# Moving the context key and value products of the joint attention behind the latent feed-forward

## The chip, the cores and the metric

One Trainium2 chip, one NeuronCore of it. A core has TensorE (PE: matrix products from SBUF into PSUM), VectorE (DVE), ScalarE (ACT) and GpSimd (POOL), each with its own in-order instruction queue, and SyncE (SP), whose queue issues most of the DMAs. SBUF is the working memory; PSUM has eight banks of 128 partitions by 2 KB. Engines wait for each other through semaphores only. The metric is the device time of one execution in microseconds (us), the median of three runs.

## The reference

Two networks in a row on 512 tokens of width 1024, everything in float32. The first block runs two layers, each with a mixer (latent attention, pooling, spatial gating) and a feed-forward. In a layer's mixer, keys and values of the attention come from a normed vector of 256, and `sg_mixer` takes another projection `v` of the same rows:

```python
p = jnp.einsum('bsd,dn->bsn', rmsnorm(x, mix_norm[l]), w_in[l])
ckv = rmsnorm(h_kv, kv_norm_g)            # keys and values, a part of p
z = jax.nn.gelu(h_uv)                     # u and v of the gating, another part of p
```

The second block works on the 512 latent tokens and 256 context tokens. Its layer 0 has a recurrent mixer and a feed-forward for both; its layer 1 has a joint attention for the latents, in which the context gives keys and values only:

```python
h_lat = modulate(x, norm_g[l, 0], sh1, sc1)       # rmsnorm times gain, plus shift
h_ctx = modulate(ctx, norm_g[l, 0], csh1, csc1)
q_c, k_c, v_c = prep(h_ctx, False)                # products with w_qkv; q and k rmsnormed per head
q_l, k_l, v_l = prep(h_lat, True)                 # the same with rotary angles
k_all = jnp.concatenate([k_c, k_l], axis=1)
y_lat = blocked_attention(q_l, k_all, v_all) @ w_out
x = x + g1 * rmsnorm_2(y_lat, norm_g[l, 1])
x = x + g2 * rmsnorm_2(swiglu(modulate(x, ...), ffn_w_in[l], ffn_w_out[l]), norm_g[l, 3])
```

## The kernel before

Activations lie transposed in SBUF: a tensor is eight tiles (k = 0 to 7) of 128 features by 512 tokens (256 for the context). Each float32 operand of a product is held as two factors, a rounded one (`H`) and the rest (`L`), and each product is three matrix products: high by high, high by low, low by high.

Weights come in chunks, of 1 MB mostly. SP loads a chunk into `raw` (two buffers, by the parity of the chunk's number), ACT rounds it into `WH` (function `hi(c)`, line 844), POOL makes `WL = raw - WH` (line 773). All three have two buffers; `hi(c)` waits until PE has used chunk c-2, and SP loads chunk c when the low part of c-2 is made. The order of the chunks is one list (`names`, lines 473 to 482), which all engines follow. `rounded` (line 902) makes the high factors of a normed tensor, and its argument `late` places one `hi` among them.

The program is written out by hand per engine; there is no scheduler. A prefix names the stage: `b0`, `b1` the layers of the first block, `c` and `t` the context's and the latents' part of the recurrent layer, `k` the context's keys and values of the joint attention, `m` the joint attention and its feed-forward. Names of steps: `n1` and `n2` the norms ahead of a mixer and a feed-forward, `y1` and `y2` those behind them, `sq` squares, `sum`, `root`, `rec` and `bc` the sum over features, its root, reciprocal and spread to all partitions. The statistics of a norm go ACT (square), PE (sum by a product with ones), ACT (root), DVE (reciprocal), PE (spread, lines 3070 and 3147), DVE (the normed tensor).

Around the change:

- The latent feed-forward `t` has 22 tiles of gate and up products in four quarters (6, 6, 6, 4), and behind each quarter the down products. `key_values` exists as a generator on PE, ACT and DVE, and one step of it is taken after each tile of the last quarters. On PE it has the 96 products of the context's keys (48, into bank `S[0]`) and values (48, into `S[1]`), each 128 by 256, ahead of the last quarter's down products, and then the sums and the spread of the keys' norm between these. Its two weight chunks `k.kv` come ahead of the last down chunks `t.dn3`.
- Behind the feed-forward PE takes the statistics of `t.y2`; DVE adds the normed result to `xT` in 8 pairs of instructions (`add_to`, line 2418: a product into `ht`, a sum into `xT`); ACT squares each new tile, PE sums the squares (`row_sums`, line 3100), and the norm `m.n1` follows. Its opening (line 3014) takes products tile by tile as the factors `hH` and `hL` come. Where PE would wait it multiplies identity matrices (`keep_busy`, line 3053, the rows with `SS<-ident`).
- In `first_mixing` of the layers `b0` and `b1` PE projects the gating's `v` in four parts (24 products each, 128 by 256, into `G[0]` to `G[3]`), with `spread_roots("nkv")` between the second and third.
- At the norm `t.n1` of the latents in the recurrent layer, ACT makes `hi` of the second column chunk ahead of the first high factor.

## Time and profile before

| what | value |
|---|---|
| median of three runs | 3058.39 us (3052.99 to 3061.25) |
| the profiled execution | 3058.06 us, of which its span 3056.3 us |
| mean granted TensorE clock | 0.989 of full |
| PE, busy | 2979.7 us, 97% |
| PE, weight loads | 2479.6 us, 81% |
| DVE, ACT, POOL busy | 56%, 39%, 40% |
| DMA | 323.81 MB, mean 106 GB/s |

The share of PE in the chain that ended last is 89%, that of DVE 7%. Times in the trace are counted from the start of the span; 1.8 us of the execution lie outside it. A row that begins with a start, a length and PE stands for one instruction or for several merged ones (`x16`, weight loads counted beside products). A matmul's length holds the way through the array, so the time that one takes of the engine is the distance to the next start. In brackets is the idle time of the engine ahead of the row, and what ended it. The granted clock has two levels here, 2.4 and 1.2 GHz.

### The profile page before, as it was taken

To read this page: it belongs to the slowest core of one execution; us is meant where nothing else is said; L and a number is where in the kernel's file an instruction comes from. 1 tells how busy PE (TensorE), PEld (TensorE's weight loads), DVE (VectorE), ACT (ScalarE), POOL (GpSimd) and SP (SyncE) were. 2 spreads that over 40 slices of the span, in tenths; PEclk is the share of its full clock that TensorE was granted. 3 is DMA by queue.
4 is the path that set the end of the run, shared out by engine and by line. 5 is a ranking of instruction groups with operands and counts; after the bars stand their busy time and mean duration, and the time that the engine had idled before them with its cause. 6 is when DMAs were issued, how large, how long until landed. Compare 5 with 4: busy or idle time off the path is not lost.

```text
span 3056.3 us, 41128 instructions
## 1 busy us (share of the span) xinstructions
PE 2979.7 (97%) x16292; PEld 2479.6 (81%) x16292; DVE 1718.6 (56%) x2812; ACT 1180.8 (39%) x1826; POOL 1237.1 (40%) x584
## 2 busy tenths in 40 slices
PE   8999999999999999999999999999999999999999
PEld 7668888776688888888888998878878779888887
DVE  4656677846563553654428866676684478431113
ACT  4553222246445333234436655531223445332222
POOL 4223444532276333324444554444444320244442
PEclk9999999999999999999999999999999999999999
DMA  7214554522245223223333343355653220123331
GB/s 133 66 56 128 167 174 149 174 63 68 75 132 148 87 70 93 74 68 132 106 90 99 115 124 105 124 153 170 199 161 110 70 69 1 42 76 102 100 98 67
DMA packets 468112, 323.81 MB, mean 106 GB/s; under 512 B 90200, under 2 KB 435424, under 8 KB 467408
## 3 DMA queue, kind: packets, MB, share of 16 engines
q1 hardware_dynamic: 463152, 309.55, 34.4%
q10 hardware_dynamic: 2656, 6.30, 0.6%
q0 software_dynamic: 2112, 5.32, 0.5%
q8 instruction: 130, 2.13, 0.3%
q14 instruction: 62, 0.51, 0.1%
HBM read 315.85 MB, written 5.24 MB: 105 GB/s over the span
## 4 chain that ended last, share of the span: by engine, by line
PE 89%; DVE 7%; ACT 2%; issue 1%; POOL 1%; DMA 0%; DVEq 0%; ACTq 0%; POOLq 0%
PE G L2997 13%; PE G L3006 13%; PE G L3007 12%; PE G L3011 12%; PE G L3252 6%; PE G L3253 5%; PE G L3257 5%; PE G L3024 3%; PE G L4173 1%; PE SS L3381 1%; PE G L3487 1%; PE MM L3381 1%; PE G L3473 1%; DVE acc L1783 1%; PE G L3418 1%
## 5 line engine op out<-in xcount | busy, mean ns | idle before, releaser
L773 POOL TENSOR_TENSOR WL<-raw,WH 128x1024 fp32r<-128x1024 f32 (+1 forms) x520 | 1194.1, 2318 | 1709.0 <-ACT WH L844 1709.0
L844 ACT ACTIVATE WH<-raw 128x1024 fp32r<-128x1024 f32 (+1 forms) x520 | 493.2, 996 | 582.4 <-PE G L3257 374.4
L3006 PE MATMUL G<-hH,WH 128*128 128x512 f32 x1520 | 595.2, 392 | 0.7 <-ACT xtok L1583 0.7
L3007 PE MATMUL G<-hL,WH 128*128 128x512 f32 x1520 | 591.9, 389 | 0.0
L3011 PE MATMUL G<-hH,WL 128*128 128x512 f32 x1520 | 359.9, 389 | 0.0
L3006 PEld LDWEIGHTS G<-hH,WH 128*128 128x128 f32 x1520 | 285.4, 188 | 64.6 <-issue 3.3
L3011 PEld LDWEIGHTS G<-hH,WL 128*128 128x128 f32 x1520 | 285.3, 188 | 59.2
L3007 PEld LDWEIGHTS G<-hL,WH 128*128 128x128 f32 x1520 | 285.4, 188 | 58.4
L1783 DVE SCALAR_TENSOR_TENSOR acc<-adaw,cvec,acc 128x512 f32<-128x512 f32 x280 | 286.4, 1075 | 4.2
L1812 DVE TENSOR_TENSOR FH<-silu,G 128x512 fp32r<-128x512 f32 x44 | 30.2, 687 | 234.2 <-PE G L3011 178.6
L2997 PE MATMUL G<-hH,WH 128*128 128x512 f32 (+1 forms) x416 | 160.0, 385 | 0.0
L2997 PE MATMUL G<-hL,WH 128*128 128x512 f32 (+1 forms) x416 | 157.4, 378 | 0.0
L2997 PE MATMUL G<-hH,WL 128*128 128x512 f32 (+1 forms) x416 | 157.3, 378 | 0.0
L3252 PE MATMUL G<-FH,WH 128*128 128x512 f32 x352 | 140.6, 399 | 0.3 <-DVE xT L1828 0.3
L3253 PE MATMUL G<-FL,WH 128*128 128x512 f32 x352 | 138.2, 392 | 0.0
L928 ACT ACTIVATE silu<-G 128x512 f32<-128x512 f32 x44 | 26.3, 598 | 274.0 <-PE G L3011 265.0
L1812 DVE TENSOR_TENSOR m_FH<-m_silu,G 128x512 fp32r<-128x512 f32 x22 | 15.1, 687 | 188.9 <-PE G L3011 183.3
L2997 PEld LDWEIGHTS G<-hH,WH 128*128 128x128 f32 x416 | 79.0, 190 | 15.2 <-issue 1.1
L2997 PEld LDWEIGHTS G<-hL,WH 128*128 128x128 f32 x416 | 79.0, 190 | 14.6 <-issue 0.7
L2997 PEld LDWEIGHTS G<-hH,WL 128*128 128x128 f32 x416 | 78.8, 189 | 14.5
L3257 PE MATMUL G<-FH,WL 128*128 128x512 f32 x352 | 85.0, 389 | 0.0
L3024 PE MATMUL G<-hH,WH 128*128 128x512 f32 (+1 forms) x160 | 65.3, 408 | 17.7 <-DVE hL L2464 7.6
(832 smaller groups left out, 5973.6 us busy)
## 6 DMA issues: line engine op xcount, KB each, us to landing
raw<-ffn_w_in_in SPq DMA_DIRECT2D x264, 256.0 KB, 3.4
adaw<-ada_w_in SPq DMA_DIRECT2D x48, 1024.0 KB, 5.2
raw<-ab_w_in_in SPq DMA_DIRECT2D x128, 256.0 KB, 3.0
raw<-ffn_w_out_in SPq DMA_DIRECT2D x96, 256.0 KB, 2.9
raw<-w_gate_in SPq DMA_DIRECT2D x88, 256.0 KB, 3.3
raw<-w_up_in SPq DMA_DIRECT2D x88, 256.0 KB, 3.4
raw<-w_down_in SPq DMA_DIRECT2D x64, 256.0 KB, 3.0
raw<-w_in_in SPq DMA_DIRECT2D x40, 256.0 KB, 3.7
```

Source lines behind the costliest of these rows:

```text
L773: nc.gpsimd.tensor_tensor(low(c)[:, cut], raw[c % 2][:, cut], high(c)[:, cut].bitcast(F32), ALU.subtract)\
L844: nc.scalar.activation(high(c)[:, cut], raw[c % 2][:, cut], ACT.Copy).then_inc(weights_hi, 1)
L1783: V.scalar_tensor_tensor(sums[:, b, i, :], weights[h % 2][:, k, :], col, sums[:, b, i, :], ALU.mult, ALU.add)\
L2997: last = mm(dst, x, y, start=(k == 0 and j == 0), stop=(k == K - 1 and j == 2))
L3006: mm(dst, view(high(c), k), xh, start=(k == 0 and not (joint and i)), stop=False)
L3007: mm(dst, view(high(c), k), xl, start=False, stop=False)
L3011: last = mm(dst, view(low(c), k), X(k)[0], start=False, stop=(k == K - 1 and not (joint and i == 0)))
L3024: last = mm(dst, x, y, start=(k == order[0] and j == 0 and not (joint and i)), stop=(k == K - 1 and j == 2 and not (joint and i == 0)))
L3252: mm(dst, part(high(c), k, cols, o), xh, start=(k == 0 and not (joint and i)), stop=False)
L3253: mm(dst, part(high(c), k, cols, o), xl, start=False, stop=False)
L3257: last = mm(dst, part(low(c), k, cols, o), X(k)[0], start=False, stop=(k == count - 1 and not (joint and i == 0)))
L3381: mm(SCORES[i][:, :], qT[:, h, i * P:i * P + P], kT[:, h, :], start=True, stop=True).then_inc(pe_done, did("pe", f"{n}.sc{4 * h + i}"))
```

## The change

- Order of chunks: `k.kv` comes behind `t.dn3`, and ahead of `m.qkv`.
- PE: the 96 products leave the generator. `sums_with_keys` issues them one by one (`fill`) behind the feed-forward: 24 ahead of the sums of `t.y2`, 6 ahead of its spread, 18 behind it, then 4 behind each of the eight row sums of `m.n1`, 6 ahead of its column sums, 6 behind them and 4 behind its spread. The keys go to `S[1]`, the values to `G[2]`. The identity products of these places go; the eight ahead of the opening stay.
- The keys' norm: its sums follow the opening of `m.qkv` on PE, its spread and DVE's products lie in the second head pair; the factors `c_kH` and `c_kL` are made one pair later.
- ACT: `hi(k.kv + 1)` comes behind the last square of `t.y2`, `hi(m.qkv)` behind the second square of `m.n1`, `hi(m.qkv + 1)` ahead of the fourth high factor (before: ahead of the first). The copies of the keys out of PSUM come behind the fifth square, those of the values behind the sixth high factor.
- DVE: the product of each pair in `add_to("t", 2)` goes to PSUM (`G[0]`, `G[3]`) in place of `ht`.
- `first_mixing`: `spread_roots("nkv")` is moved from the third `v` part to the fourth.
- `t.n1`: `hi` of the second column chunk is moved from the first high factor to the third.

In three places the order of the instructions is shown, as a listing of the two programs has it (engine's order, line, operation, output and inputs, shape). On PE, from the end of the latent feed-forward to the second row sum of `m.n1`, before:

```order
L3257 MATMUL G<-t_FH,WL_68 128x512 x8
L3059 MATMUL SS<-ident 128x128 x8
L3092 MATMUL MM<-ones,rstd 128x1 x4
L3095 MATMUL MM<-ones,sq 128x1 x4
L3059 MATMUL SS<-ident 128x128 x2
L3147 MATMUL MM<-ident,ncol 128x128 x4
L3059 MATMUL SS<-ident 128x128 x8
L3103 MATMUL MM<-sq,ones 1x512
L3059 MATMUL SS<-ident 128x128
```

And in the changed kernel (`c_kH`, `c_kL` are the factors of the normed context, `WH_54` and `WH_57` the two weight buffers):

```order
L3263 MATMUL G<-t_FH,WL_68 128x512 x8
L3980 MATMUL SS<-c_kH,WH_54 128x256
...
L3098 MATMUL MM<-ones,rstd 128x1 x4
L3101 MATMUL MM<-ones,sq 128x1 x4
L3980 MATMUL SS<-c_kH,WH_54 128x256
...
L3153 MATMUL MM<-ident,ncol 128x128 x4
L3980 MATMUL SS<-c_kH,WH_54 128x256
...
L3109 MATMUL MM<-sq,ones 1x512
L3994 MATMUL G<-WH_57,c_kH 128x256
L3994 MATMUL G<-WL_68,c_kH 128x256
L3994 MATMUL G<-WH_57,c_kL 128x256
L3994 MATMUL G<-WH_57,c_kH 128x256
```

The identity products are gone, context products stand in their places, and four of the values' products follow the first row sum. On ACT, from the end of the feed-forward to the high factors of `m.n1`, before:

```order
L844 ACTIVATE WH_54<-raw_52 128x1024 x2
L870 ACT_TABLE_LOAD
L870 ACTIVATE MM<-MM,eps 128x4
L894 ACTIVATE rstd<-t_y_181 128x512
L894 ACTIVATE sq<-t_y_181 128x512 x7
L870 ACTIVATE MM<-MM,eps 128x4
L853 ACTIVATE sq<-xT 128x512 x8
L861 ACTIVATE rstd<-MM 1x512
L870 ACTIVATE ncol<-MM,eps 128x4
L844 ACTIVATE WH_57<-raw_53 128x1024 x2
L911 ACTIVATE hH<-SS,mod 128x512
L911 ACTIVATE hH<-MM,mod 128x512
```

And in the changed kernel:

```order
L890 ACTIVATE sq<-t_y_181 128x512 x7
L840 ACTIVATE WH_57<-raw_53 128x1024 x2
L866 ACT_TABLE_LOAD
L866 ACTIVATE MM<-MM,eps 128x4
L849 ACTIVATE sq<-xT 128x512 x2
L840 ACTIVATE WH_54<-raw_52 128x1024 x2
L849 ACTIVATE sq<-xT 128x512 x3
L1542 ACTIVATE kc<-SS 128x256 x2
L849 ACTIVATE sq<-xT 128x512 x3
...
L866 ACTIVATE ncol<-MM,eps 128x4
...
L913 ACTIVATE hH<-SS,mod 128x512
L840 ACTIVATE WH_57<-raw_53 128x1024 x2
```

The table load and a pair of weight halves now stand behind the last square of `t.y2`, another pair behind the second square of `m.n1`, and the third pair, which stood ahead of the first high factor, behind the third. On PE in layer `b0` (and alike in `b1`), around the spread of `nkv`, with the banks' numbers, before:

```order
L2997 MATMUL G1<-WL0_62,hH_50 128x256
L2997 MATMUL G1<-WH0_54,hL_51 128x256
L3070 MATMUL MM<-nrow_89,ident_77 128x128 x4
L2997 MATMUL G2<-WH0_54,hH_50 128x256
L2997 MATMUL G2<-WL0_62,hH_50 128x256
```

And in the changed kernel:

```order
L3003 MATMUL G2<-WL0_62,hH_50 128x256
L3003 MATMUL G2<-WH0_54,hL_51 128x256
L3076 MATMUL MM<-nrow_89,ident_77 128x128 x4
L3003 MATMUL G3<-WH0_54,hH_50 128x256
L3003 MATMUL G3<-WL0_62,hH_50 128x256
```

The spread now stands ahead of the part that goes to `G3`, 24 products later than before.

The diff, cut to its core and without its repeated parts:

```diff
@@ -476,8 +476,7 @@
         names += [("c.o", 4, SLOT), *columns_of("t"), *halves("c"), ("t.o", 4, SLOT)]
-        latent = halves("t")
-        names += [*latent[:-1], ("k.kv", 2, SLOT), latent[-1]]
+        names += [*halves("t"), ("k.kv", 2, SLOT)]
         names += [("m.qkv", 6, SLOT), ("m.o", 4, SLOT)]
@@ -896,6 +892,12 @@
                     (added_square if n in ADDED else square)(n, k, src(k), fresh)
+                    if n == "t.y2" and k == K - 1:
+                        hi(first["k.kv"] + 1)
+                    if n == "m.n1" and k == 1:
+                        hi(first["m.qkv"])
+                    if n == "m.n1" and k == 4:
+                        keys_out()
                 stats_before[0] = f"{n}.sum"
@@ -1532,23 +1534,18 @@
                 rounded("k.n1", KD, PC.kH, None, TC, shift("k", 0), temp=sq)
-                yield
-                c = first["k.kv"]
-                hi(c + 2)
+            def keys_out():
                 for g in range(2):
                     act.wait_ge(pe_done, at("pe", "k.k1"))
-                    nc.scalar.activation(kc[:, g, :], S[0][:, g * TC:g * TC + TC], ACT.Copy).then_inc(act_done, did("act", f"k.k{g}"))
-                hi(c + 3)
+                    nc.scalar.activation(kc[:, g, :], S[1][:, g * TC:g * TC + TC], ACT.Copy).then_inc(act_done, did("act", f"k.k{g}"))
+            def values_out():
                 for k in range(TC // P):
                     act.wait_ge(pe_done, at("pe", "k.v1"))
-                    nc.scalar.activation(vc[:, k, :], S[1][:, k * 2 * P:k * 2 * P + 2 * P], ACT.Copy).then_inc(act_done, did("act", f"k.v{k}"))
-                yield
-                act.wait_ge(act_done, at("act", "k.k1"))
-                act.wait_ge(dve_done, at("dve", f"k.n1.L{KD - 1}"))
-                nc.scalar.activation(sq[:, 0, :], kc[:, :, :].rearrange("p g t -> p (g t)"), ACT.Square).then_inc(act_done, did("act", "k.nk.sq"))
-                yield
-                root("k.nk", 2 * (TC // P), P)
-                stats_before[0] = "k.nk.sum"
+                    nc.scalar.activation(vc[:, k, :], G[2][:, k * 2 * P:k * 2 * P + 2 * P], ACT.Copy).then_inc(act_done, did("act", f"k.v{k}"))
 
@@ -1593,7 +1590,7 @@
             projected("c", PC.y, TC, KD, ((3, final_roots), (5, lambda: turned_context(2))))
-            rounded("t.n1", KD, hH, f"c.o{KD - 1}", T, shift("t", 0), late=first["t.ab"] + 1)
+            rounded("t.n1", KD, hH, f"c.o{KD - 1}", T, shift("t", 0), late=first["t.ab"] + 1, late_at=2)
             turned_context(3)
@@ -1607,7 +1604,10 @@
             stats("m.n1", KD, lambda k: xT[:, k, :], lambda k: act.wait_ge(dve_done, at("dve", f"t.x2.{k}")))
-            rounded("m.n1", KD, hH, f"t.up{FT - 1}", T, shift("m", 0), late=first["m.qkv"] + 1)
+            rounded("m.n1", KD, hH, f"t.up{FT - 1}", T, shift("m", 0), late=first["m.qkv"] + 1, late_at=3, then=lambda k: values_out() if k == 3 else None)
+            act.wait_ge(act_done, at("act", "k.k1"))
+            nc.scalar.activation(sq[:, 0, :], kc[:, :, :].rearrange("p g t -> p (g t)"), ACT.Square).then_inc(act_done, did("act", "k.nk.sq"))
+            stats_before[0] = "k.nk.sum"
             c = first["m.qkv"]
@@ -1634,14 +1634,17 @@
 
-            for g in range(2):
-                act.wait_ge(dve_done, at("dve", f"k.kn{g}"))
-                nc.scalar.activation(c_kH[:, g, :], kc[:, g, :], ACT.Copy).then_inc(act_done, did("act", f"m.cH{g}"))
             for i in range(NH // 2):
...
                     root(f"m.p{i - 1}", 2 * P, P)
+                else:
+                    root("k.nk", 2 * (TC // P), P)
                 head(2 * i + 1)
+                if i == 1:
+                    for g in range(2):
+                        act.wait_ge(dve_done, at("dve", f"k.kn{g}"))
+                        nc.scalar.activation(c_kH[:, g, :], kc[:, g, :], ACT.Copy).then_inc(act_done, did("act", f"m.cH{g}"))
                 hi(c + 2 + i)
@@ -2419,14 +2422,15 @@
                     dve.wait_ge(dve_done, here())
-                    V.scalar_tensor_tensor(temp[:, k % 2, 0:N], y[:, k, :], g(k), bank[:, 0:N], ALU.mult, ALU.mult)\
+                    step = (G[0], G[3])[k % 2][:, 0:N] if (n, which) == ("t", 2) else temp[:, k % 2, 0:N]
+                    V.scalar_tensor_tensor(step, y[:, k, :], g(k), bank[:, 0:N], ALU.mult, ALU.mult)\
                         .then_inc(dve_done, did("dve", f"{n}.d{which}.{k}"))
...
                     dve.wait_ge(dve_done, here())
-                    V.tensor_tensor(x[:, k, :], x[:, k, :], temp[:, k % 2, 0:N], ALU.add).then_inc(dve_done, did("dve", f"{n}.x{which}.{k}"))
+                    V.tensor_tensor(x[:, k, :], x[:, k, :], step, ALU.add).then_inc(dve_done, did("dve", f"{n}.x{which}.{k}"))
 
@@ -3308,8 +3314,9 @@
                     if k == 2:
+                        pe.wait_ge(act_done, at("act", f"{n}.prow1"))
+                    if k == 3:
                         spread_roots(f"{n}.nkv")
-                        pe.wait_ge(act_done, at("act", f"{n}.prow1"))
                     cut = bass.ds(k * P, P)
@@ -3959,28 +3966,74 @@
                 yield
+            def key_products():
                 c = first["k.kv"]
-                X = features(PC.kH, PC.kL, TC)
                 ready("k.n1", KD)
...
                 for g in range(2):
-                    three(S[0][:, g * TC:g * TC + TC], KD, weights_of(c, blocks(2 * P)(g)), X).then_inc(pe_done, did("pe", f"k.k{g}"))
-                tally.also("pe", f"used.{c}")
+                    weights = weights_of(c, blocks(2 * P)(g))
+                    for q in range(KD):
+                        (wh, wl), (xh, xl) = weights(q), (PC.kH[:, q, :], PC.kL[:, q, :])
+                        for j, (x, y) in enumerate(((wh, xh), (wh, xl), (wl, xh))):
+                            last = mm(S[1][:, g * TC:g * TC + TC], x, y, start=(q == 0 and j == 0), stop=(q == KD - 1 and j == 2))
+                            if q == KD - 1 and j == 2:
+                                last.then_inc(pe_done, did("pe", f"k.k{g}"))
+                            if g == 1 and q == KD - 1 and j == 2:
+                                tally.also("pe", f"used.{c}")
+                            yield
                 chunk(c + 1)
+                pe.wait_ge(dve_done, at("dve", "t.down3.6"))
+                weights = weights_of(c + 1, lambda w, q: w[:, q * 2 * P:(q + 1) * 2 * P])
                 for k in range(TC // P):
                     cut = bass.ds(k * P, P)
-                    three(S[1][:, k * 2 * P:k * 2 * P + 2 * P], KD, lambda q: (PC.kH[:, q, cut], PC.kL[:, q, cut]),
-                          weights_of(c + 1, lambda w, q: w[:, q * 2 * P:(q + 1) * 2 * P])).then_inc(pe_done, did("pe", f"k.v{k}"))
-                tally.also("pe", f"used.{c + 1}")
-                yield
-                yield
+                    for q in range(KD):
+                        (wh, wl), (xh, xl) = weights(q), (PC.kH[:, q, cut], PC.kL[:, q, cut])
+                        for j, (x, y) in enumerate(((xh, wh), (xh, wl), (xl, wh))):
+                            last = mm(G[2][:, k * 2 * P:k * 2 * P + 2 * P], x, y, start=(q == 0 and j == 0), stop=(q == KD - 1 and j == 2))
+                            if q == KD - 1 and j == 2:
+                                last.then_inc(pe_done, did("pe", f"k.v{k}"))
+                            if k == 1 and q == KD - 1 and j == 2:
+                                tally.also("pe", f"used.{c + 1}")
+                            yield
+            def fill(products, count):
+                for _ in range(count):
+                    next(products, None)
+            def sums_with_keys():
+                products = key_products()
+                fill(products, 24)
+                pe.wait_ge(dve_done, at("dve", stats_before[0]))
+                added_columns("t.y2", KD)
+                fill(products, 6)
+                pe.wait_ge(dve_done, at("dve", "t.y2.rec"))
+                to_all(M[1][:, :], 0).then_inc(pe_done, did("pe", "t.y2.bc"))
+                fill(products, 18)
+                for k in range(KD):
+                    row_sums("m.n1", k)
+                    fill(products, 4)
+                fill(products, 6)
+                row_columns("m.n1")
+                fill(products, 6)
+                pe.wait_ge(dve_done, at("dve", "m.n1.rec"))
+                to_all(M[1][:, :], 0).then_inc(pe_done, did("pe", "m.n1.bc"))
+                fill(products, 4)
+                stats_before[0] = "m.n1.rec"
+            def keys_sum():
                 pe.wait_ge(act_done, at("act", "k.nk.sq"))
-                pe.wait_ge(dve_done, at("dve", stats_before[0]))
                 for t in range(4):
...
                 stats_before[0] = "k.nk.rec"
-                yield
+            def keys_root():
                 pe.wait_ge(dve_done, at("dve", "k.nk.rec"))
@@ -4130,6 +4183,8 @@
                     if b == 0:
+                        if i == 1:
+                            keys_root()
                         head_sums(i - 1)
...
                             swap(i - 2)

```

## Rows read from the trace of the kernel before

**Rows 1.** The page's first part: engine, busy us (share), instructions.
```profile
PE 2979.7 (97%) x16292; PEld 2479.6 (81%) x16292; DVE 1718.6 (56%) x2812; ACT 1180.8 (39%) x1826; POOL 1237.1 (40%) x584
```

**Rows 2.** Instructions in time order (start us, length us, engine, idle before), PE, key products.
```profile
2351.26 3.79 PE L3011 MATMUL G<-hH,WL 128*128 128x512 f32 x16
2355.43 0.35 PE L2997 MATMUL SS<-c_kH,WH 128*128 128x256 f32 x1 [0.38 <-ACT ht L928]
...
2366.88 0.39 PE L3252 MATMUL G<-t_FH,WH 128*128 128x512 f32 x1
```

**Rows 3.** Instructions in time order, VectorE, beside those products.
```profile
2356.78 0.69 DVE L1815 TENSOR_TENSOR t_FL<-G,t_FH 128x512 fp32r<-128x512 f32 x1
```

**Rows 4.** Instructions in time order, PE, from the latent feed-forward's end to the opening.
```profile
2391.58 2.02 PE L3059 MATMUL SS<-ident 128*128 128x128 f32 x16 [0.87 <-DVE t_y L1828]
...
2395.83 1.16 PE L3147 MATMUL MM<-ident,ncol 128*128 128x128 f32 x8
...
2409.77 1.02 PE L3103 MATMUL MM<-sq,ones 128*1 128x512 f32 x2
2410.72 0.49 PE L3059 MATMUL SS<-ident 128*128 128x128 f32 x2
2411.47 1.05 PE L3109 MATMUL MM<-ones,rstd 1*128 1x1 f32 x8 [0.26 <-ACT rstd L861]
...
2416.68 0.47 PE L3024 MATMUL G<-hH,WH 128*128 128x512 f32 x1 [0.66 <-ACT hH L911]
```

**Rows 5.** Instructions in time order, ScalarE, same stretch.
```profile
2391.47 0.63 ACT L894 ACTIVATE sq<-t_y 128x512 f32<-128x512 f32 x1 [0.28 <-DVE t_y L1828]
...
2401.55 0.63 ACT L853 ACTIVATE sq<-xT 128x512 f32<-128x512 f32 x1 [0.88 <-DVE xT L2429]
...
2417.36 0.69 ACT L911 ACTIVATE hH<-SS,mod 128x512 fp32r<-128x512 f32 x1 [0.82 <-DVE SS L1750]
```

**Rows 6.** Instructions in time order, PE, value products of layers 0 and 1.
```profile
79.51 1.16 PE L3070 MATMUL MM<-nrow,ident 128*128 128x128 f32 x8 [3.40 <-DVE nrow L1723]
...
677.66 1.17 PE L3070 MATMUL MM<-nrow,ident 128*128 128x128 f32 x8 [3.39 <-DVE nrow L1723]
```

**Rows 7.** Instructions in time order, ScalarE and PE, opening of the latent columns.
```profile
1425.21 1.99 ACT L844 ACTIVATE WH<-raw 128x1024 fp32r<-128x1024 f32 x2
...
1428.71 0.47 PE L3024 MATMUL G<-hH,WH 128*128 128x512 f32 x1 [3.82 <-POOL WL L773]
```

**Rows 8.** The chain of waits (start us, length us, what).
```profile
80.67 5.76 PE G L2997 x48
...
678.83 7.23 PE G L2997 x48
...
1428.71 12.78 PE G L3024 x48
```

**Rows 9.** Instructions in time order, ScalarE: a table load ahead of a root.
```profile
1373.71 1.28 ACT L870 ACT_TABLE_LOAD   x1
1375.16 0.25 ACT L870 ACTIVATE SS<-SS,eps 128x16 f32<-128x16 f32 x1 [0.16 <-PE SS L3701]
```

**Rows 10.** Instructions in time order, VectorE, same stretch.
```profile
2420.13 0.74 DVE L1739 SCALAR_TENSOR_TENSOR hL<-MM,mod,hH 128x512 fp32r<-128x512 f32 x1
```

**Rows 11.** Instructions in time order, GpSimd, around the opening.
```profile
2413.84 4.71 POOL L773 TENSOR_TENSOR WL<-raw,WH 128x1024 fp32r<-128x1024 f32 x2 [29.93 <-ACT WH L844]
```

**Rows 12.** Instructions on one tile, the rotary table swap: its load.
```profile
DMA to landing us min/median/max: 4.5/4.5/4.5
```

**Rows 13.** Instructions of one line: ns min/median/max, first and last start, shape.
```profile
L1828 DVE TENSOR_TENSOR xT<-xT,G x64: 686/687/691, 315.4 to 1389.3; 128x512 f32<-128x512 f32 x64
...
L2429 DVE TENSOR_TENSOR ctxT<-ctxT,ht x8: 424/425/1932, 1478.3 to 1488.7; 128x256 f32<-128x256 f32 x8
```
**Rows 14.** Gating of `b0` in time order: DVE's last product on v, PE's first use.
```profile
93.43 1.23 DVE L1926 TENSOR_TENSOR vg<-vg,sgrow 128x1024 f32<-128x1024 f32 x1
...
109.29 1.12 PE L3355 MATMUL MM<-b_s,bsel 33*128 33x512 f32 x2
```

24 lines of the change are left out of this document (11 added, 13 removed).

## The prediction

> **What bounds the kernel now.** I read the page first: PE is busy for 97% of the span [rows 1], while its weight loads fill 81%. So nothing is gained beside PE; time can only come from work that PE no longer does on its own account, from waits of PE, and from stretches in which it runs at the lower clock. Then I read the time-ordered views of the four places that the change touches, and looked there for idle time in brackets. Three things are to be seen.
>
> (a) The 96 context products stand alone on PE between the last up product and the first down product: from the idle 0.38 us ahead of 2355.43 to 2366.88 [rows 2], 11.83 us, or 0.119 us a product. Nothing but DVE's last low factor (from 2356.78, 0.69 us long [rows 3]) is under way beside them.
>
> (b) Behind the feed-forward, from 2391.58 to 2416.68 [rows 4], PE waits for a chain through DVE and ACT: sums, root, eight tiles at 1.51 us each (ACT's square 0.63 us and its idle 0.88 us [rows 5]), sums, root, first factors. Of this PE's share is small, and identity products fill the rest. That stretch is 25.1 us long, the products need 11.4.
>
> (c) In `b0` and `b1` PE idles 3.40 and 3.39 us ahead of the spread of `nkv` [rows 6], and at `t.n1` 3.82 us ahead of the opening [rows 7]. The stretches behind two of these are slow: 48 products of 256 columns take 5.76 us in `b0` and 7.23 us in `b1` [rows 8].
>
> **Part 1, the products leave the feed-forward's end.** The down products then start 11.83 us earlier. What is late next: they need the latest low factor of the feed-forward only at their 13th product. A product of 512 columns takes 0.23 us (16 in 3.79 [rows 2]), so that is 2.7 us after their start at about 2355.0, at 2357.7; DVE has it at 2356.78 + 0.69 = 2357.47 [rows 3]. The cover is 0.2 us; I count no wait. The sums and the spread of the keys' norm also leave the down products and come back one for one among the latents' heads: 0. Removed: **11.8 us**.
>
> **Part 2, the products go between the statistics.** They cost only where they or their companions are longer than what they stand beside. All that follows is serial, so lateness adds up.
> - First fill: 24 products, 24 x 0.119 = 2.9 us, for eight identity products of 1.9 us (2.02 with the way through the array [rows 4]). The sum of `t.y2` comes 1.0 later. Six products (0.8) stand for two identities (0.6) ahead of the spread, whose reciprocal comes late by the same 1.0: +0.1.
> - ACT's table load moves to just ahead of this root. At 1373.71 such a load ran before the wait of its root ended: it took 1.28 us, and the root still waited 0.16 us for PE [rows 9]. Here ACT ends its last square at 2392.1 (2391.47 + 0.63 [rows 5]); with 2.0 for the weight halves and 1.3 for the load it is ready at 2395.4. The root is wanted 0.5 ahead of the old spread (2395.83 [rows 4]) plus 1.0, at 2396.3. Hidden.
> - `hi(m.qkv)` behind the second square is 2.0 us long (1.99 [rows 7]) in a queue that has 0.88 us free in a step [rows 5]. The third square comes 2.0 - 0.9 = 1.1 to 1.2 late. ACT then catches up, PE doesn't: a row sum takes 0.95 of PE (2409.77 to 2410.72 [rows 4]), four products 0.48 and the change back to them some 0.08, together 1.51 us, just the pace of DVE's step. So the last row sum is **1.2** late.
> - Behind the last row sum PE issues ten products before the column sums: 0.95 + 1.28 = 2.23, where before 1.70 went by (2409.77 to 2411.47): +0.5. Six instead of two identities ahead of the second spread: +0.2. Four more ahead of the opening: 0.5 of the 0.66 us for which PE idled [rows 4]: 0.
> - `hi(m.qkv + 1)` now delays the fourth high factor. The third is written 2417.36 to 2418.05 [rows 5], then 2.0 us of weights and 0.7 of the factor, to 2420.8; DVE took that factor at 2420.13 [rows 10], and PE follows DVE tile by tile: +0.7.
> - The loads of the rotary tables stand on POOL behind the low part of that chunk. It ran from 2413.84 for 4.71 us [rows 11]; it would now start at 2419.2, the last load be issued at 2424.9 and land 4.5 later [rows 12], at 2429.4. PE waits for it behind the opening and the keys' sums, at about 2429.6. Hidden with 0.2 to spare; I count 0 and keep up to 2 for the range.
>
> Sum of this part: 1.0 + 0.1 + 1.2 + 0.5 + 0.2 + 0.7 = **3.7 us back**.
>
> **Part 3, the product of each pair in PSUM.** DVE's instruction lengths for one operand in PSUM: 0.686 to 0.691 over 64 instructions, also while POOL makes low parts; a sum of two SBUF tiles beside POOL (`ctxT`, 256 columns) takes 0.42 but once 1.93 [rows 13]. Before, POOL was quiet for 29.9 us ahead of 2413.84 [rows 11]; now two low parts, four instructions, lie beside DVE's pairs. With the product in PSUM I count 0; bounds: -0.5 if the pair gets shorter, and 4 x 1.5 = 6.0 if each of POOL's four instructions stops DVE once. Zero is next to the row with PSUM.
> The Trainium skill (SBUF — State Buffer, section "Who interferes with whom") has this as a rule: a VectorE instruction with two SBUF inputs contends with a GpSimd instruction that reads SBUF, and one with at most one does not. By that rule the sum has 0 here, and would have up to 6.0 more with `ht` kept; the rows agree with it.
>
> **Part 4, the spread of `nkv`.** The 24 products (2.9 us at 0.120) now run where PE idled 3.40 and 3.39 us; 0.5 us of the wait is left, the spread comes when it came, and PE is 2.9 earlier behind it: 2 x 2.85 = **5.7 us**. What is next late: DVE's work on `v` ended at 93.43 + 1.23 = 94.7 and PE wanted it at 109.29 [rows 14], 14.6 us later; it has slack for all of it. Behind the wait in `b1` the same 48 products took longer than in `b0`, at the lower clock for a part; with 0.5 us of idleness I expect it not to fall: 7.23 - 5.76 = **1.5 us**. In `b0` a wait as long left the clock up, so this is likely and not sure.
>
> **Part 5, `t.n1`.** The first high factor waited behind `hi` (1425.21, 1.99 us [rows 7]). Now it starts at 1425.3, and PE's opening at 1426.8 in place of 1428.71: 1.9. The `hi` comes before the third factor, which costs 0.4. The opening itself took 12.78 us [rows 8], against 48 x 0.23 = 11.0: 1.7 at the lower clock behind an idle time of 3.82. With 2.0 us of it left I count 1.0 of that: 1.9 - 0.4 + 1.0 = **2.5 us** (bounds 1.0 and 3.2).
>
> **The sum.** Against the profiled execution: 3058.06 - 11.8 + 3.7 - 5.7 - 1.5 - 2.5 = 3058.06 - 17.8 = 3040.3 us. The median of the runs is 0.33 above that execution, so 3040.6; I say **3040.5 us**, 0.59% below.
>
> **Rivals.**
> - *The chain in the seam is longer than counted.* For: PE's and DVE's pace in the row sums are equal to 0.01 us, the cover of the tables' load is 0.2 us, and each late item adds up. If the row-sum step takes 1.8 us, 8 x 0.3 = 2.4 more; with 2 us of waiting for the tables, 1 for a POOL stop, and 1.5 for the clock kept low in `b1`: 3040.5 + 6.9 = about 3047.5. Against: each step has a row of its own length.
> - *The waits in `b0`, `b1` and `t.n1` come back later.* For: PE at 97% [rows 1] leaves hardly any waits to see, so the slack of the others isn't visible either. Then only parts 1 and 2 count: 3058.4 - 8.1 = 3050.3, no measurable change. Against: everything behind these places is released relative to PE, DVE and ACT start as much earlier, and no load or clock of its own holds them.
> - *DVE's pairs in PSUM are stopped, slower in the end.* Place: the 16 instructions of `add_to` between the spread and the last row sum. Price 1.5 us for each one stopped [rows 13]. All 16 would be 24 us: 3040.5 + 24 = 3064.5. It decides from 12 stopped on (18 us). For: `G[0]` and `G[3]` are PSUM banks beside the one that PE now fills, and POOL works beside it. Against: 64 instructions of that kind never went over 0.691, and POOL has only four instructions there.
> - *The change does not do what it says:* PE might still wait for the products' weights. The tightest are those of the values: `hi(k.kv + 1)` runs behind the square that ends at 2392.1, the first low half starts at 2393.2 and POOL takes 4.7 us [rows 11], to 2397.9; the 49th product follows the first row sum at about 2401. If they came 4 us late, 1 us; I leave it inside the range.
>
> **How the numbers follow.** My forecast 73%, the longer seam 14%, the waits that come back 10%, PSUM 3%. What this kernel's measurement can tell from no change is 0.3%, 9.2 us, that is 3049.2. The forecast's own range is 3035 to 3046: from all of part 2 hidden (3036.8) and the clock's gifts larger by 2, to the clock gains of 2.5 absent and 3 of spread between runs. Towards the rivals I take 3034 to 3050. Faster by over 0.3%: 0.73 + 0.12 + 0.01 = 0.86; same: 0.02 + 0.09 = 0.11; slower 0.03.
>
> **What would show it.** In the profile of the changed kernel: the down products of the last quarter directly behind the last up product, with no idle time (part 1); from the end of the last down product to the opening some 29 us in place of 25 to 26, with the third square of `xT` late by 1.2 and the last row sum still so (part 2); DVE's pairs at 0.75 and 0.69 us beside POOL (part 3); waits of 0.5 us ahead of the spreads of `nkv`, and 48 products behind none of them slow (part 4); the opening of `t.n1` 2 us after the last product before it (part 5). I am wrong if PE's idle time grows elsewhere by more than 3 us, if the seam takes over 33 us, or if the low clock shows in new places.

## The result and the profile after

| | before | after |
|---|---|---|
| median, first comparison | 3059.19 us (4 runs, 3052.99 to 3061.25) | 3034.45 us (4 runs, 3031.76 to 3036.84) |
| ratio, 95% interval | | 0.9922 [0.9904, 0.9940] |
| repeated later, median | 3057.45 us (9 runs) | 3037.80 us (5 runs) |
| ratio, 95% interval | | 0.9938 [0.9924, 0.9951] |
| profiled execution; its span | 3058.06; 3056.3 us | 3032.47; 3030.7 us |
| mean granted clock in it | 0.989 | 0.992 |

The change makes the kernel 0.6 to 0.8% faster. The forecast was 3040.5 us (0.59% less), with a range of 3034 to 3050: the sign and the mechanism are right, and the measured gain is larger. All 9 runs of the changed kernel together have a mean of 3035.9 us, the 46 runs of the kernel before 3058.4: 22.5 us less, good to about 2 us by the spread of the runs, where the sum said 17.8.

The page after [rows 1]: PE is busy for 2961.0 us in place of 2979.7.

```profile
PE 2961.0 (98%) x16236; PEld 2462.2 (81%) x16236; DVE 1721.3 (57%) x2812; ACT 1179.5 (39%) x1826; POOL 1237.6 (41%) x584
```

PE in time order, from the last up products to the products behind the opening (start, length, engine, line, ...; in brackets the idle time before it). It answers to [rows 2, 4]:

```profile
2335.73 3.79 PE L3017 MATMUL G<-hH,WL 128*128 128x512 f32 x16
2339.35 0.39 PE L3258 MATMUL G<-t_FH,WH 128*128 128x512 f32 x1
...
2362.25 0.36 PE L3980 MATMUL SS<-c_kH,WH 128*128 128x256 f32 x1 [0.90 <-DVE t_y L1831]
...
2365.16 0.95 PE L3098 MATMUL MM<-ones,rstd 128*128 128x1 f32 x8
...
2367.66 1.05 PE L3153 MATMUL MM<-ident,ncol 128*128 128x128 f32 x8
...
2370.94 1.02 PE L3109 MATMUL MM<-sq,ones 128*1 128x512 f32 x2 [0.18 <-ACT sq L849]
...
2372.56 1.02 PE L3109 MATMUL MM<-sq,ones 128*1 128x512 f32 x2
...
2374.87 1.02 PE L3109 MATMUL MM<-sq,ones 128*1 128x512 f32 x2 [0.64 <-ACT sq L849]
...
2382.97 1.02 PE L3109 MATMUL MM<-sq,ones 128*1 128x512 f32 x2
...
2385.29 1.05 PE L3115 MATMUL MM<-ones,rstd 1*128 1x1 f32 x8
...
2387.09 1.05 PE L3153 MATMUL MM<-ident,ncol 128*128 128x128 f32 x8
...
2390.59 0.47 PE L3030 MATMUL G<-hH,WH 128*128 128x512 f32 x1 [0.19 <-ACT hH L913]
...
2402.52 0.95 PE L4031 MATMUL MM<-ones,sq 128*128 128x1 f32 x8
```

The down products follow the last up product (2335.73 + 16 x 0.227 = 2339.35) with no idle time. From the first fill (2362.25) to the opening (2390.59) are 28.34 us; before it was 25.10 [rows 4]. The third row sum waited 0.64 us for its square (2374.87), and from then on the row sums are 1.62 us apart, where before they were 1.51 apart. Four more rows of the kernel before are needed for the terms below: its sum of `t.y2`, its first row sum, its second spread, and the first product behind its opening.

```profile
2393.44 0.95 PE L3092 MATMUL MM<-ones,rstd 128*128 128x1 f32 x8
...
2399.31 1.02 PE L3103 MATMUL MM<-sq,ones 128*1 128x512 f32 x2 [0.53 <-DVE ht L2422]
...
2413.08 1.16 PE L3147 MATMUL MM<-ident,ncol 128*128 128x128 f32 x8
...
2428.16 0.39 PE L2997 MATMUL G<-hH,WH 128*128 128x512 f32 x1
```

The eighth row sum came 10.46 us after the first (2399.31 to 2409.77) and comes 12.03 after it now (2370.94 to 2382.97). The opening took 11.48 us (2416.68 to 2428.16) and takes 11.93 (2390.59 to 2402.52). ScalarE and GpSimd beside it; the two long ACT rows are the chunks that were moved there [rows 5, 7, 11]:

```profile
2372.31 1.99 ACT L840 ACTIVATE WH<-raw 128x1024 fp32r<-128x1024 f32 x2
2374.20 1.22 ACT L849 ACTIVATE sq<-xT 128x512 f32<-128x512 f32 x2
...
2391.85 2.00 ACT L840 ACTIVATE WH<-raw 128x1024 fp32r<-128x1024 f32 x2
...
2373.43 4.71 POOL L769 TENSOR_TENSOR WL<-raw,WH 128x1024 fp32r<-128x1024 f32 x2 [4.89 <-ACT WH L840]
```

The two spreads of `nkv` and the opening of `t.n1` [rows 6 to 8]. The idle time ahead of them is 0.52, 0.52 and 1.93 us; before it was 3.40, 3.39 and 3.82:

```profile
76.92 1.16 PE L3076 MATMUL MM<-nrow,ident 128*128 128x128 f32 x8 [0.52 <-DVE nrow L1726]
...
672.22 1.16 PE L3076 MATMUL MM<-nrow,ident 128*128 128x128 f32 x8 [0.52 <-DVE nrow L1726]
...
1416.45 0.47 PE L3030 MATMUL G<-hH,WH 128*128 128x512 f32 x1 [1.93 <-DVE hL L1742]
```

### The profile page after: what moved, and what is told of

The parts are those of the page before. It is cut to its first block, busy times and chain, and to the rows that moved or that the text cites. A ratio compares the mean times of both kernels' runs of the same rounds, so it can differ in the third digit from the quotient of the medians.

```text
span 3030.7 us, 41013 instructions
## 1 busy us (share of the span) xinstructions
PE 2961.0 (98%) x16236; PEld 2462.2 (81%) x16236; DVE 1721.3 (57%) x2812; ACT 1179.5 (39%) x1826; POOL 1237.6 (41%) x584
## 4 chain that ended last, share of the span: by engine, by line
PE 89%; DVE 7%; ACT 2%; issue 1%; POOL 1%; DMA 0%; DVEq 0%; ACTq 0%; POOLq 0%
PE G L3003 13%; PE G L3012 13%; PE G L3013 13%; PE G L3017 13%; PE G L3258 5%; PE G L3259 5%; PE G L3263 5%; PE G L3030 3%; PE G L4228 1%; PE SS L3388 1%; PE G L3494 1%; PE MM L3388 1%; PE G L3480 1%; DVE acc L1786 1%; PE G L3832 1%
## 5 line engine op out<-in xcount | busy, mean ns | idle before, releaser
L3003 PE MATMUL G<-hH,WH 128*128 128x512 f32 (+1 forms) x416 | 160.1, 385 | 0.0
L3258 PEld LDWEIGHTS G<-FH,WH 128*128 128x128 f32 x352 | 66.6, 189 | 18.2 <-issue 1.8
```

Source lines behind the costliest of these rows:

```text
L3003: last = mm(dst, x, y, start=(k == 0 and j == 0), stop=(k == K - 1 and j == 2))
L3258: mm(dst, part(high(c), k, cols, o), xh, start=(k == 0 and not (joint and i)), stop=False)
```

## Where the time went

I laid the two traces over each other: the same instruction is looked up in both, and the difference of its start is followed through the program. Each step in it is a place where time went.

| place | step after minus before, us | forecast |
|---|---|---|
| the start, ahead of any edit | -2.5 | 0 |
| spread of `nkv`, `b0` | -3.0 | -2.85 |
| spread of `nkv`, `b1`, clock included | -4.3 | -4.35 |
| opening of `t.n1` | -1.9 | -1.5 |
| its length (12.78 both times) | 0.0 | -1.0 |
| behind 1920 and behind 2000 (before's times) | -2.4, -0.9 | 0 |
| last up product to first down product | -12.0 | -11.8 |
| keys' norm out of the down products | -1.8 | among the heads one for one |
| first fill to the opening | +3.2 | +3.0 |
| the opening itself | +0.45 | +0.7 |
| keys' norm among the heads | +1.8 | |
| behind 2655 | -2.2 | 0 |
| all others, single steps of up to 1.5 of both signs | 0.0 | 0 |

The rows with a forecast sum to -17.6; the parts that were counted came out within 0.5 us each, except the clock of `t.n1`. The other -8 us stand at places that no edit touches. There the same instructions are under way, at another clock. The largest of the steps that cancel is such a place too: 3.4 us at the low clock at 888 us of the changed kernel cost 1.5, where the kernel before has none, and the slow stretch at 853 us of the kernel before is shorter in the changed one, for about as much. Two places of the -8 us by windows (window, length, PE busy (instructions), granted clock, DMA share, GB/s); first before, then after:

```profile
5.00:30.00 25.00, 20.37 (x107) 0.93 1.01 213
1980.00:2010.00 30.00, 25.99 (x133) 0.77 0.00 1
```

```profile
5.00:30.00 25.00, 20.04 (x118) 1.00 1.00 214
1965.00:1995.00 30.00, 24.88 (x137) 0.89 0.00 1
```

## The experiments

**1. Parts 4 and 5 alone.** To the kernel before:

```diff
@@ first_mixing, PE @@
                     if k == 2:
-                        spread_roots(f"{n}.nkv")
                         pe.wait_ge(act_done, at("act", f"{n}.prow1"))
+                    if k == 3:
+                        spread_roots(f"{n}.nkv")
@@ t.n1, ACT @@
-            rounded("t.n1", ..., late=first["t.ab"] + 1)
+            rounded("t.n1", ..., late=first["t.ab"] + 1, late_at=2)
```

> The kernel before with parts 4 and 5 alone (the spread of nkv one value product group later in b0 and b1, the second weight chunk of t.n1 ahead of the third high factor). Theory (waits given back for good, each -2.88 in b0 and -2.88 in b1, and -1.9 at t.n1): the program behind t.n1 runs 7.7 us earlier than before, -9.2 with the slow stretch behind the wait of b1 gone; time about 3059.2 - 9 = 3050. Rival (the waits come back later as other waits): shift of the last third back near 0, time 3059. Rival (the clock, not the waits, is what differed between the two executions): the shifts at places that no edit touches (start of the program, 1850 to 1942 us, 2660 us) differ again, by other amounts and signs than in the changed kernel, 1 to 3 us at a place.

Measured: 3044.51 us (5 runs) against 3057.07 (9), ratio 0.9955 [0.9942, 0.9967]. The steps are -2.95, -4.3 and -1.9, as the theory has them, and nothing comes back: "the waits come back" falls. But 3057.07 - 3044.51 = 12.6 us, 3.4 more than the 9.2 counted. In the trace this excess is once more at untouched places: -2.2 at 1942 us and -0.9 at 2009. The second rival, that the clock at untouched places would differ by other amounts and signs than in the changed kernel, is borne out in half: these two steps are the same in both, but the start (0 here, -2.5 there) and the place behind 2655 us (+0.4 here, -2.2 there) differ.

**2. Parts 1 to 3 alone**: the changed kernel with the two edits of experiment 1 taken back.

> The changed kernel with parts 4 and 5 undone, so parts 1 to 3 alone. Theory (12.0 us of products taken out of the feed-forward's end, 3.7 given back between the statistics): the opening of m.n1 stands 8.3 us earlier than before relative to the last up product, PE idles 3.4 us ahead of both spreads of nkv and 3.8 ahead of the opening of t.n1; time about 3059.2 - 8.3 = 3051. Rival (the two halves help each other, by the clock or by earlier loads): less than 8 from the seam, time 3053 or more, and the two halves together less than the changed kernel's 24.7. By the theory the halves sum to 17.4 and the remaining 7 are the granted clock of the executions.

Measured: 3046.79 us (5 runs), ratio 0.9965 [0.9952, 0.9977], 10.3 us by medians. The step from the last up product to behind the heads' first products is -8.4 us in the trace. The halves add up within their spread: 12.6 + 10.3 = 22.9 by medians and 24.3 by means, the whole change has 22.5 by its mean. In this kernel the waits of `b0` and `b1` are there again (3.4 us); the spreads behind them took 2.08 and 1.52 us, against 1.16 at the high clock, and the 48 products 6.17 and 6.92.

**3. The kernel before, a second time.**

> The kernel before, unchanged, profiled a second time. Theory (the 8 us beyond the counted parts are the granted clock, whose slow stretches fall in other places from one execution to the next): the program is the same, yet stretches of PE at the lower clock stand in other places than in the first profile, with shifts of 1 to 3 us at single places and the mean clock between 0.989 and 0.992. Rival (the slow stretches belong to the program): the same places as in the first profile, shifts under 0.5 us everywhere.

The chain of waits (start, length, what), two rows of the first execution, to which the 5.76 us at 80.67 of [rows 8] belong, and four of the second:

```profile
90.30 19.07 PE G L2997 x84
...
1942.34 4.97 DVE hL L2819 x2
```

```profile
80.03 2.07 PE MM L3070 x8
82.10 6.19 PE G L2997 x48
92.16 19.07 PE G L2997 x84
...
1941.85 4.98 DVE hL L2819 x2
```

One program, and yet it is 1.9 us behind itself at 92 us and 0.5 ahead at 1942. Behind the wait of `b0` the spread and the products together took 1.16 + 5.76 = 6.92 us in one [rows 6, 8] and 2.07 + 6.19 = 8.26 in the other: 1.3 us for the low clock. So the prediction's "in `b0` a wait as long left the clock up" held for the one execution that it was read from. The theory stands in part: of the slow stretches most have the same place in both executions, and some come, go or change their length, a microsecond or two at a place.

**4. The changed kernel, a second time**, five runs.

> The changed kernel, unchanged, timed and profiled again beside the version with halves. Theory (between executions of one program the low clock falls in other places): stretches at the start, behind 1400 us, at 1930 us and behind 2640 us differ from the first profile by 0.5 to 2.5 us each, while the seam from the last down product to the end of the opening is the same to 0.2 us; median 3034 to 3037. Rival (the first profile's places are fixed by the program): all shifts under 0.5 us.

Measured: 3037.80 us, 3033.65 to 3039.16, 0.8 above the range expected. In the traces it is 3.4 us later than the first from 35 us on, 1.2 later from 1437 us on, and has no lasting step over 0.15 us from there to the end; the seam is the same to 0.1 us. The theory's places were too many: differences at the start and at 840 to 1440 us, none at 1930 and 2640. That the mean clock is 0.992 in both profiles of the changed kernel, and 0.989 and 0.988 in both of the kernel before, says that a part of the 8 us is the change's after all. The sums of (1 - granted clock) x length over the profiles say the same: 35.1 and 35.5 us before, 25.3 and 25.3 after. Four profiles are few, and both of the changed kernel are of executions faster than its mean. But every run has its granted clock listed: (1 - clock) x span has a mean of 35.8 us over 42 runs of the kernel before (those of the first comparison have none) and of 28.7 over the 9 of the changed one. That is 7.1 us less at the low clock, and 15.4 of the 22.5 us are left for the work.

**5. Is it PE's idle time that brings the low clock?** The kernel before, with every wait where it was, but identity products in it:

```diff
                     if k == 2:
-                        spread_roots(f"{n}.nkv")
                         pe.wait_ge(act_done, at("act", f"{n}.prow1"))
+                        for _ in range(13):
+                            mm(G[3][:, 0:P], ident[:, :], ident[:, :], start=True, stop=True)
+                        spread_roots(f"{n}.nkv")
...
+            for _ in range(15):
+                mm(G[0][:, 0:P], ident[:, :], ident[:, :], start=True, stop=True)
             columns(PT_, hH, hL, "t.n1", ...
```

> The kernel before, with the waits as they were, but PE multiplies identity matrices in them: thirteen (3.1 us) in the 3.40 us ahead of each spread of nkv, fifteen (3.6 us) in the 3.82 us ahead of the opening of t.n1. It separates the clock from the work: nothing is taken off PE's path. Theory (the low clock behind these waits comes from PE's idle time): the 48 products behind the wait of b1 take 5.8 us in place of 7.23, the opening of t.n1 11.3 in place of 12.78, with the pieces later in the program unchanged: 2 to 4 us faster than before, 3054 to 3056. Rival (the low clock stands where it stands, or moves to the next stretch): the slow pieces come back within a few us of the places, time 3058 within its spread.

Measured: 3054.89 us (11 runs) against 3058.51 (15), 3.6 us less by medians; the ratio, 0.9984 [0.9975, 0.9993], stands for 4.9 us with an interval of 2 to 8, for multiplying nothing. The chain:

```profile
77.62 5.75 PE G L2997 x48
...
675.85 5.76 PE G L2997 x48
...
1423.46 11.65 PE G L3024 x48
```

Against [rows 8] it is 5.76 for 7.23 and 11.65 for 12.78. That is 2.6 us, and 1.3 more in the executions in which `b0` is slow too (experiment 3): 2.6 to 3.9, which explains what was measured. All 13 traces answer the question together. Counted is whether a slow stretch follows:

| wait of PE | left idle | filled with identity products |
|---|---|---|
| 3.40 us, spreads of `nkv` in `b0` and `b1` | 5 of 6 | 0 of 2 |
| 0.52 us, the same spreads with part 4 | 0 of 18 | |
| 3.82 us, opening of `t.n1` | 3 of 3 | 0 of 1 |
| 1.93 us, the same opening with part 5 | 4 of 8 | 0 of 1 |

So it is the idle time of PE that brings the low clock at these places; at 1.93 us it does so in half of the executions. For the changed kernel this gives, beside the work, 1.5 us in `b1`, 1.3 in `b0` in two of three traces, and 1.0 at `t.n1` in half of them.

**6. The same for the changed kernel**: eight identity products in the 1.93 us that are left ahead of the opening of `t.n1`.

> The changed kernel with eight identity products (1.95 us) where PE idles 1.93 us ahead of the opening of t.n1. Theory C (the low clock in the opening follows that idle time): the 48 products take 11.3 us instead of 12.78, everything behind is 1.4 us earlier. Rival D (the low clock there doesn't hang on this idle time; a fully busy stretch at 1400 to 1403 us had it too): the opening still takes 12.5 or more, or another stretch near it is slow, and nothing is gained, 0.1 lost.

One execution: 3032.07 us, clock 0.994. From the start of the opening to the next instruction behind it went 11.7 us instead of 12.6. By itself this settles nothing, because in experiment 7, which has no such products, the same stretch behind the same 1.93 us of idle time also took 11.7. The opening in the chain of the changed kernel and of experiment 7:

```profile
1416.45 12.78 PE G L3030 x48
```

```profile
1418.46 11.81 PE G L3030 x48
```

The distance from its third product to its fourth is 0.43 us in one and 0.23 in the other. An idle time of 1.9 us is followed by the low clock at times, in 4 of 8 traces by the table above. That is why the 1.0 us forecast for this opening was there in some executions and not in the profiled one.

**7. The late third square or PE's pace?** The changed kernel with the rounding of the first joint-attention chunk behind the last square:

```diff
-                    if n == "m.n1" and k == 1:
+                    if n == "m.n1" and k == K - 1:
                         hi(first["m.qkv"])
```

> The changed kernel with the rounding of the first joint-attention chunk behind the last square of m.n1 instead of the second. Theory A (PE's own pace decides: 1.62 us for a row sum and four products, above DVE's 1.51): the third row sum is no longer late, the eighth follows the first by 7 x 1.62 = 11.34 us instead of 12.03, and the opening comes 0.7 us earlier. Rival B (the late third square is passed on in full, as the prediction had it): the eighth row sum follows the first by 10.6 to 10.8, and the opening comes 1.2 to 1.5 us earlier.

**8. Three products a step**, and both edits together:

```diff
                 for k in range(KD):
                     row_sums("m.n1", k)
-                    fill(products, 4)
-                fill(products, 6)
+                    fill(products, 3)
+                fill(products, 3)
                 row_columns("m.n1")
-                fill(products, 6)
+                fill(products, 4)
...
-                fill(products, 4)
+                fill(products, 17)
```

The eight identity products ahead of the opening are left out too.

> The changed kernel with three products behind each row sum instead of four, three more behind the last, four ahead of the second spread, and the remaining seventeen in place of the identity products ahead of the opening; the rounding stays behind the second square. Theory A (PE's pace decides): with three products the pace falls to about 1.50, PE catches up with the squares although the third is late, the eighth row sum follows the first by 10.6 us instead of 12.03; with 0.6 less behind the last row sum and 0.2 less ahead of the spread the opening comes 2.2 us earlier. Rival B (the late square is passed on): only the 0.8 behind the last row sum and the 0.5 of pace are gained, 1.3.

> The last two edits together. Theory A: as fewer_per_step, the opening 2.2 us earlier and nothing from the place of the rounding. Rival B: 0.9 more than fewer_per_step. Time by A: about 3034.5 - 2.2 = 3032.3. What could go against it: the second chunk's rounding waits for the last value product, which now ends 2 us ahead of the opening, and the loads behind the first chunk's low part start 8 us later, for which PE would wait 0 to 4 us among the heads.

The first and the eighth row sum of the three (experiment 7, three products, both):

```profile
2372.23 1.02 PE L3109 MATMUL MM<-sq,ones 128*1 128x512 f32 x2 [0.18 <-ACT sq L849]
...
2383.57 1.02 PE L3109 MATMUL MM<-sq,ones 128*1 128x512 f32 x2
```

```profile
2375.82 1.02 PE L3109 MATMUL MM<-sq,ones 128*1 128x512 f32 x2 [0.18 <-ACT sq L849]
...
2379.75 1.02 PE L3109 MATMUL MM<-sq,ones 128*1 128x512 f32 x2 [0.85 <-ACT sq L849]
...
2387.25 1.02 PE L3109 MATMUL MM<-sq,ones 128*1 128x512 f32 x2
```

```profile
2371.05 1.02 PE L3109 MATMUL MM<-sq,ones 128*1 128x512 f32 x2 [0.17 <-ACT sq L849]
...
2381.64 1.02 PE L3109 MATMUL MM<-sq,ones 128*1 128x512 f32 x2
...
2384.01 1.05 PE L3115 MATMUL MM<-ones,rstd 1*128 1x1 f32 x8 [0.44 <-ACT rstd L857]
```

| | rounding behind second square | behind last |
|---|---|---|
| four products a step | 12.03 | 11.34 |
| three products a step | 11.43 | 10.59 |

The table has the time from the first to the eighth row sum, in us. With four, PE's own pace of 1.62 decides and the place of the rounding is worth 0.7, as theory A said. With three, A was wrong, and rival B right: PE's step of 1.50 is no shorter than DVE's 1.51, so it has nothing to catch up with, and the late square (0.85 of waiting at 2379.75) is passed on in full. From the first fill to the opening (the first fill counted at its 2.91) the four kernels take 28.3, 27.6, 27.2 and 26.9 us. In the last one the rounding stands in the way of the copy of the row sums: PE waits 0.44 for it (2384.01). The time can't show so little: 3033.99 and 3037.25 (one run each) and 3036.59 (5 runs, ratio 0.9929 [0.9916, 0.9943]).

**9. A version from these rows.** Both chunks in halves of 1.0 us, which fit a step of ScalarE nearly whole, and the products spread by PE's idle time:

```diff
-                    if n == "m.n1" and k == 1:
-                        hi(first["m.qkv"])
+                    if n == "m.n1" and k in (1, 3):
+                        hi(first["m.qkv"], k // 2)
...
-                fill(products, 24)
+                fill(products, 21)
...
+                    fill(products, 3)
+                fill(products, 2)
                 row_columns("m.n1")
+                fill(products, 4)
...
+                fill(products, 21)
```

The second chunk's halves stand ahead of the third and the fifth high factor, and the eight identity products ahead of the opening are left out.

> The changed kernel with three products behind each row sum, the products spread 21, 6, 18, 8 x 3, 2, 4, 21, no identity products ahead of the opening, and both joint-attention chunks rounded in halves of 1.0 us, ahead of the third and fifth square (in a queue with 0.88 us free a step, so 0.1 late each) and ahead of the third and fifth high factor. Theory A (pace and late square are the two costs, and a half chunk hides in one step): the eighth row sum 10.6 to 10.8 us after the first in place of 12.03, the column sums 1.75 behind it (2.32), the first sums 0.35 earlier, the opening itself 11.5 in place of 11.93; from the last down product to the end of the opening 2.8 us less than in the changed kernel, time 3034.5 - 2.8 = about 3032. Rival (two halves cost as much as one chunk, or the opening waits for the products put ahead of it): 1.6 or less gained, as in the kernel with both edits.

```profile
2374.31 1.02 PE L3115 MATMUL MM<-sq,ones 128*1 128x512 f32 x2 [0.17 <-ACT sq L852]
...
2385.04 1.02 PE L3115 MATMUL MM<-sq,ones 128*1 128x512 f32 x2
...
2386.78 1.05 PE L3121 MATMUL MM<-ones,rstd 1*128 1x1 f32 x8
...
2392.00 0.47 PE L3036 MATMUL G<-hH,WH 128*128 128x512 f32 x1
...
2403.49 0.95 PE L4037 MATMUL MM<-ones,sq 128*128 128x1 f32 x8
```

The eighth row sum comes 10.73 after the first, the column sums 1.74 behind it, and the opening takes 11.49, as before the change. The step from ahead of the seam to behind it is -2.84 us against the changed kernel, as forecast, and the rival falls. Its time is 3035.71 us (5 runs, ratio to before 0.9930 [0.9918, 0.9943]); the changed kernel of experiment 4, timed beside it, has 3037.80, 0.9938 [0.9924, 0.9951]. It is the better version by the trace; by the medians it is 2.1 us faster and by the means 1.4, but the intervals overlap.

**10. Part 3, the other way.** The changed kernel with the product of each pair in `ht`:

```diff
-                    step = (G[0], G[3])[k % 2][:, 0:N] if (n, which) == ("t", 2) else temp[:, k % 2, 0:N]
+                    step = temp[:, k % 2, 0:N]
```

> The changed kernel with the product of each pair of the last residual in ht (SBUF) again. Theory of part 3 (an SBUF sum of two tiles stands back behind a POOL instruction that reads SBUF): of the 16 DVE instructions of the pairs, one or two beside POOL's low part (two instructions of 2.35 us) take 1.5 us longer each, the last row sum comes 1.5 to 3 us later, time 3036 to 3038. Rival (the bank makes no difference): all pairs at 0.75 and 0.69 us, time unchanged at 3034.5 within its spread.

VectorE and GpSimd, fourth and fifth pair:

```profile
2377.93 0.75 DVE L2426 SCALAR_TENSOR_TENSOR ht<-t_y,mcols,MM 128x512 f32<-128x512 f32 x1
2378.71 2.27 DVE L2433 TENSOR_TENSOR xT<-xT,ht 128x512 f32<-128x512 f32 x1
...
2381.80 1.95 DVE L2433 TENSOR_TENSOR xT<-xT,ht 128x512 f32<-128x512 f32 x1
...
2378.07 5.12 POOL L769 TENSOR_TENSOR WL<-raw,WH 128x1024 fp32r<-128x1024 f32 x2 [4.80 <-ACT WH L840]
```

Each of GpSimd's two instructions stopped one sum of two SBUF tiles (2.27 and 1.95 us in place of 0.69), and no product, which reads the spread from PSUM (0.75). In the changed kernel all 16 lie at 0.76 and 0.69 beside the same low part (2373.43 above). The stops cost DVE 2.8 us, of which 1.6 reach the opening, because PE was behind DVE by then. The time is 3037.77 us (5 runs, ratio 0.9934 [0.9921, 0.9948]); their mean, 3038.9, is 2.9 above that of the changed kernel, which the intervals of the two don't tell apart; the trace does. So the theory holds, at 2.8 us of DVE's time where the prediction's bound was 6.0. That bound had four instructions of GpSimd beside the pairs; only the two of one low part lie there. Those of the other run from 2363.84 to 2368.53 in the changed kernel, ahead of the first pair at 2368.75. The Trainium skill's rule (SBUF — State Buffer, "Who interferes with whom") marks the sum, which has two SBUF inputs, as the one of the pair that contends with GpSimd, and not the product, which has one; the trace agrees in both kernels.

## Why the prediction was right, and what was off

- **Part 1** (-11.8): right, -12.0; the idle 0.38 us ahead of the products went with them. DVE's low factor was in time: it ended at 2341.95, and the 13th product stands at 2342.07, so the cover was 0.1 us where 0.2 was counted.
- **Part 2** (+3.7): right as a sum, 3.24 to the opening and 0.45 in it. Its terms, forecast and measured by the starts above against [rows 4]: first fill 1.0 and 1.05, second 0.1 and 0.11, behind the last row sum 0.5 and 0.62, second spread 0.2 and 0.19, fourth high factor 0.7 and 0.45. For the row sums 1.2 was forecast and 1.57 measured; 0.2 ahead of them and 0.1 ahead of the opening came back. Here a step was wrong: "together 1.51 us, just the pace of DVE's step". It is 1.62 (2370.94 to 2372.56): 0.95 for the row sum and 0.67, not 0.56, for four products with the changes to them and back. Experiments 7 and 8 show both causes apart.
- **Part 3** (0): right; experiment 10 gives the other end, 2.8 us at DVE and 1.6 at the opening. The prediction put both low parts beside the pairs; only one lies there.
- **Part 4** (-5.7 and -1.5): right. Waits of 0.52 us ahead of the spreads, -3.0 and -4.3 at the places. The reading that the clock stays up behind the wait of `b0` held in one trace of three; in the other two the low clock cost 1.3 us there, which the sum has at nothing.
- **Part 5** (-2.5): the opening came 1.9 earlier, at 1426.8 by the clock of before, as forecast; the second high chunk cost nothing to see where 0.4 was counted, and the 1.0 for the clock was not there in the profiled execution. The "1.7 at the lower clock" was read too high: with the wait filled and the clock up the opening takes 11.65 us (experiment 5) and not 48 x 0.23 = 11.0, so the low clock costs 1.1 of its 12.78.
- **What was too small** is the granted clock. The prediction counted 2.5 us for it, at two places. The kernel as a whole has 22.5 us less, the counted work is 17.6 - 1.5 = 16.1, so about 6 us are the clock; the clock listed with every run says 7.1. Some 3 of them come from the waits that the change shortens: 1.5 in `b1`, 1.3 in `b0` in two of three traces, 1.0 at `t.n1` in half. The remaining 3 to 4 us, with 2 of uncertainty in the 22.5, come from places without an edit (behind 1920, 2000 and 2655 us in the profiled one), where the slow stretches were fewer or shorter. Why they fell and didn't rise isn't shown. That the first median, 3034.45, still lies inside the range of 3034 to 3050, if only just, is owed to the room left for a larger gift of the clock, and not to a term of the sum.
- **Its own signs of being wrong.** The seam took 29 us and not 33, and PE's idle time fell from 76.6 to 69.7 us of the span, 8.0 at the places counted, so it grew by 1.1 elsewhere. The third sign, a low clock in a new place, did appear once (at 888 us), and cost nothing in the end, because another slow stretch was as much shorter.
- **The rivals.** "The waits come back" fell with experiment 1, "pairs stopped" with experiment 10, late weights with the trace (no such wait of PE). "The longer seam" was half true: a step of 1.62 in place of the 1.51 counted and the 1.8 it supposed. The row sums took 0.4 us more than counted, and the seam as a whole came out at the forecast 3.7.

## What to carry to other kernels

Filling a wait with work from elsewhere pays the work's full length only if each piece is no longer than what it stands beside: measure the step of each engine in such a chain, the change from one kind of product to another included. Leave a margin: four products fitted the step by the sum to 0.01 us and didn't in fact, three did. A rounding that shares a queue with the chain is best cut into pieces of about the queue's free time in one step; halves of 1.0 us in a queue with 0.88 free delayed the third row sum by 0.2 us, the whole of 2.0 us by 0.8. An idle PE can cost more than its idle time, here up to 1.5 us behind a wait of 3.4 and 1.0 behind one of 1.9; where nothing useful fits a wait, empty products do.

## What the runs showed of the hardware

- The lower level of TensorE's clock is granted in stretches of some 3 to 10 us, 12 to 14 of them in each of the four profiles of the two kernels; (1 - granted clock) x length of all of them is 25.3 to 35.5 us there. Two executions of one program differ by 1 to 3 us at a place (experiments 3 and 4). Most of the spread between runs goes with it: over the 42 runs of the kernel before with a listed clock, from 3052.69 to 3065.83 us, the time and (1 - clock) x span have a correlation of 0.85. So a difference under 3 us is read from the trace of one stretch, not from the time.
- One such stretch falls where PE has no idle time at all, in 12 of the 13 traces (not in that of experiment 5). In the changed kernel, 1400 to 1402 us (window, length, PE busy (instructions), clock, DMA share, GB/s):

```profile
1400.00:1402.00 2.00, 2.00 (x11) 0.50 0.53 145
1402.00:1404.00 2.00, 2.00 (x15) 0.70 0.75 216
```
